# A hybrid decoder step on one core: a new opening, a second query tile in the residual loop, and a down projection that keeps the tokens stationary

## The chip, the cores and the metric

The kernel runs on one core of one Trainium2 chip (trn2). The metric is device time in microseconds; three runs of the kernel before gave 3130.1, 3130.15 and 3132.04 us, median 3130.15 us.

## What is computed

One layer of a decoder on 576 tokens: 512 prompt tokens and 64 sample tokens (8 sequences of 8). The width is 2048. Cut to what matters here:

```python
def decoder_layer(x, ...):
    h = rmsnorm(x, g_mix_pre)
    rq, rk, rv, rg, dq, dk, dv = mixer_projections(h, w_in, pos)   # 2048 -> 7168
    ...                                                            # retention and differential attention
    x = x + rmsnorm(mix @ w_out, g_mix_post)
    x = x + rmsnorm(cross_attn(rmsnorm(x, g_mem_pre), mem_k, mem_v, w_mem_q, w_mem_o), g_mem_post)
    x = x + rmsnorm(sq_relu_mlp(rmsnorm(x, g_mlp_pre), w_up, w_down), g_mlp_post)

def cross_attn(h, mk, mv, wq, wo):
    q = (h @ wq)                                                   # 2048 -> 4 heads of 128
    ...

def sq_relu_mlp(h, w_up, w_down):
    return jnp.square(jax.nn.relu(h @ w_up)) @ w_down              # 2048 -> 8192 -> 2048
```

All tensors are float32.

## The kernel before

The kernel is written engine by engine: one block each for SyncE (`sp`, weight loads and most stores), GpSimd (`pool`), ScalarE (`act`), VectorE (`dve`) and TensorE (`pe`). The order on each engine is the order of its text; semaphores with written-out counts tie them.

Products with weights are made from three float32r matmuls each: a float32 operand is split into a high part (a ScalarE copy into float32r) and a low part (a VectorE subtraction), and high times high, low times high and high times low are summed in PSUM (`parts`, L1846). Weights come in stripes of 128 x 2048 values (1 MB) through two buffers: SyncE loads `w_raw`, ScalarE writes `w_hi` (`hi`, L812; L1105 and L1118 in the MLP), VectorE writes `w_lo` (`lo`, L1165), and SyncE may load a buffer again when its `w_lo` is written. ScalarE may write `w_hi` of a buffer when TensorE has finished the tiles that read it.

Activations are kept transposed: features on partitions, the 576 tokens along the free axis. The weights are the stationary operand, the tokens the moving one, in two halves of 288 columns that go to two PSUM banks. An output tile is 128 features by 576 tokens. The PSUM banks are `G[0..3]` (gemm) and `A[0..3]` (aux).

The stages that the change touches:

- The opening. GpSimd loads the token tiles (`x_load`, L629) into two buffers `xin`, then four small lambda vectors and the page table; SyncE loads the constants and the first weight stripes at once; ScalarE's queue loads the gains. TensorE turns each token tile (`x_turn`, L1867), VectorE multiplies by the gain (L1189), ScalarE writes the high part (L832), VectorE the low part (L1196), in quarters of 512 columns. The gains themselves are turned once (L1888), after all small loads, the page table included. The first two input tiles are computed in halves (`half_tile`, L1875): half 0 of tile 0 after the third token tile, half 0 of tile 1, then five small matmuls that spread the norm factor, then both second halves.
- The residual after the mixer (`residual(0, ...)`, L1606 to L1615, with `first_tile` on TensorE). For each of 16 chunks VectorE makes the new x and its low part, ScalarE the high part and the square; TensorE sums the squares with two float32 matmuls (L2218, four instructions in the trace) and runs the six matmuls of the first query tile for that chunk. The other three query tiles follow, 96 matmuls each.
- The MLP, in 8 blocks of 1024 hidden features. `up` gives 8 tiles of hidden features: VectorE makes relu times the norm factor (L1755), ScalarE squares and writes `u_hi`, VectorE `u_lo` (L1760). `down` gives 16 tiles of output features of 8 chunks each, 8 stripes of 8 chunks x 256 columns; VectorE adds each tile to `yT` (L1777).
- The end. GpSimd loads the spilled x back over `act_hi` (L794) when the last up tile is done. In the last block squares of `yT` are summed over the tiles (L1143, L1592); then TensorE sums over partitions (L2208), ScalarE takes the root (L991), VectorE the reciprocal (L1596), VectorE and GpSimd scale `yT`, VectorE adds x (L1827), TensorE turns `yT` to tokens by features in 20 pieces (L1949), ScalarE and VectorE copy the pieces out of PSUM (L1150, L1817) and SyncE stores them (L614).

## Time and profile before

| | |
|---|---|
| median of 3 runs | 3130.15 us |
| profiled execution | 3132.76 us |
| its span, first to last instruction | 3131.1 us |
| TensorE (PE) busy | 3042.4 us (97%), 22485 matmuls |
| VectorE (DVE) busy | 1301.3 us (42%) |
| ScalarE (ACT) busy | 768.9 us (25%) |
| GpSimd (POOL) busy | 165.1 us (5%) |
| mean granted TensorE clock | 0.989 |
| DMA | 355.04 MB, mean 113 GB/s |

Times within the trace are microseconds from the span's start. PE's ends are modelled and successive matmuls overlap in the record, so the pace of a stream of matmuls is read from the distance of their starts, not from the length of one.

### The profile page before, as it was taken

To read this page: it belongs to the slowest core of one execution; us is meant where nothing else is said; L and a number is where in the kernel's file an instruction comes from. 1 tells how busy PE (TensorE), PEld (TensorE's weight loads), DVE (VectorE), ACT (ScalarE), POOL (GpSimd) and SP (SyncE) were. 2 spreads that over 40 slices of the span, in tenths; PEclk is the share of its full clock that TensorE was granted. 3 is DMA by queue.
4 is the path that set the end of the run, shared out by engine and by line. 5 is a ranking of instruction groups with operands and counts; after the bars stand their busy time and mean duration, and the time that the engine had idled before them with its cause. 6 is when DMAs were issued, how large, how long until landed. Compare 5 with 4: busy or idle time off the path is not lost.

```text
span 3131.1 us, 53528 instructions
## 1 busy us (share of the span) xinstructions
PE 3042.4 (97%) x22485; PEld 2931.0 (94%) x22485; DVE 1301.3 (42%) x1860; ACT 768.9 (25%) x836; POOL 165.1 (5%) x265
## 2 busy tenths in 40 slices
PE   7999999999999998998999999999999999999996
PEld 6899999989899997787999999999999999999995
DVE  6544245445554536467332322323323233232346
ACT  4311123223222233334212112122121121221221
POOL 0000012221211010000000000000000000000001
PEclk9999999999999999999999999999999999999997
DMA  5433535554656361513222223222222222222241
GB/s 181 156 103 107 151 117 162 167 168 149 218 162 222 134 211 54 148 55 115 81 80 81 91 73 89 82 80 80 80 80 86 77 87 86 80 80 80 80 141 61
DMA packets 398904, 355.04 MB, mean 113 GB/s; under 512 B 9554, under 2 KB 362052, under 8 KB 396772
## 3 DMA queue, kind: packets, MB, share of 16 engines
q1 hardware_dynamic: 377456, 269.18, 28.7%
q0 software_dynamic: 21136, 84.66, 7.9%
q8 instruction: 56, 0.92, 0.1%
q14 instruction: 28, 0.23, 0.0%
q10 hardware_dynamic: 228, 0.06, 0.0%
HBM read 305.62 MB, written 48.23 MB: 113 GB/s over the span
## 4 chain that ended last, share of the span: by engine, by line
PE 90%; issue 4%; DVE 3%; DMA 1%; POOL 1%; ACT 1%; DVEq 0%; POOLq 0%; ACTq 0%
PE gemm L1846 81%; PE aux L1949 2%; PE gemm L1926 1%; PE gemm L1875 1%; DVE yT L1606 1%; DVE yT L1827 1%; PE aux L1989 1%; PE aux L2005 1%; DMA d_vp<-in_cache_diff_v 0%; POOL d_kp L682 0%; POOL d_vp L682 0%; ACT w_hi L812 0%; DVE rstd_b L1596 0%; DMA pg<-in_page_table 0%; PE aux L2152 0%
## 5 line engine op out<-in xcount | busy, mean ns | idle before, releaser
L1846 PE MATMUL gemm<-act_hi,w_hi 128*128 128x288 f32 x4544 | 994.8, 300 | 7.8 <-DVE act_lo L1615 4.3
L1846 PE MATMUL gemm<-act_hi,w_lo 128*128 128x288 f32 x4544 | 973.4, 296 | 0.0
L1846 PE MATMUL gemm<-act_lo,w_hi 128*128 128x288 f32 x4544 | 972.7, 296 | 0.0
L1846 PEld LDWEIGHTS gemm<-act_hi,w_hi 128*128 128x128 f32 x4544 | 731.6, 189 | 41.2 <-issue 18.1
L1846 PEld LDWEIGHTS gemm<-act_lo,w_hi 128*128 128x128 f32 x4544 | 732.6, 189 | 0.0
L1846 PEld LDWEIGHTS gemm<-act_hi,w_lo 128*128 128x128 f32 x4544 | 732.6, 189 | 0.0
L1165 DVE TENSOR_TENSOR w_lo<-w_raw,w_hi 128x2048 fp32r<-128x2048 f32 x216 | 494.4, 2289 | 198.3 <-ACT w_hi L812 74.2
L1846 PE MATMUL gemm<-u_lo,w_hi 128*128 128x288 f32 x2048 | 438.6, 296 | 0.0
L1846 PE MATMUL gemm<-u_hi,w_hi 128*128 128x288 f32 x2048 | 438.5, 296 | 0.0
L1846 PE MATMUL gemm<-u_hi,w_lo 128*128 128x288 f32 x2048 | 438.4, 296 | 0.0
L1846 PEld LDWEIGHTS gemm<-u_hi,w_hi 128*128 128x128 f32 x2048 | 330.2, 189 | 0.0
L1846 PEld LDWEIGHTS gemm<-u_lo,w_hi 128*128 128x128 f32 x2048 | 330.2, 189 | 0.0
L1846 PEld LDWEIGHTS gemm<-u_hi,w_lo 128*128 128x128 f32 x2048 | 330.2, 189 | 0.0
L812 ACT ACTIVATE w_hi<-w_raw 128x2048 fp32r<-128x2048 f32 x90 | 172.1, 1912 | 335.8 <-PE gemm L1846 280.0
L1118 ACT ACTIVATE w_hi<-w_raw 128x2048 fp32r<-128x2048 f32 x63 | 120.8, 1918 | 516.6 <-PE gemm L1846 516.6
L1777 DVE TENSOR_TENSOR yT<-yT,gemm 128x288 f32 x192 | 78.5, 450 | 362.9 <-PE gemm L1846 362.9
L1755 DVE SCALAR_TENSOR_TENSOR z_out<-gemm,rstd_b 128x288 f32<-128x288 f32 x128 | 52.6, 452 | 405.1 <-PE gemm L1846 405.0
L1110 ACT ACTIVATE z_out<-z_out 128x576 f32<-128x576 f32 x64 | 43.9, 685 | 613.8 <-DVE z_out L1755 613.8
L1105 ACT ACTIVATE w_hi<-w_raw 128x2048 fp32r<-128x2048 f32 x63 | 120.1, 1906 | 77.4 <-PE gemm L1846 76.1
L794 POOL DMA_DIRECT2D act_hi<-x_scratch x1 | 0.6, 574 | 1818.6 <-PE gemm L1846 1818.6
L1760 DVE TENSOR_TENSOR u_lo<-z_out,u_hi 128x576 f32 (+1 forms) x64 | 48.5, 758 | 112.4 <-ACT u_hi L1112 112.4
L1235 DVE TENSOR_TENSOR z_out<-gemm,rstd_b 128x288 f32<-128x288 f32 x48 | 19.7, 451 | 99.1 <-PE gemm L1846 99.1
(309 smaller groups left out, 1922.9 us busy)
## 6 DMA issues: line engine op xcount, KB each, us to landing
w_raw<-in_w_mlp_up SPq DMA_DIRECT2D x64, 1024.0 KB, 6.4
w_raw<-in_w_mlp_down SPq DMA_DIRECT2D x64, 1024.0 KB, 5.3
w_raw<-in_w_in SPq DMA_DIRECT2D x56, 1024.0 KB, 5.7
w_raw<-in_w_out SPq DMA_DIRECT2D x16, 1024.0 KB, 6.0
z_scratch<-z_out SPq DMA_DIRECT2D x56, 288.0 KB, 2.1
r_zin<-z_scratch POOLq DMA_DIRECT2D x8, 1152.0 KB, 6.3
xin<-in_x_prompt POOLq DMA_DIRECT2D x8, 1024.0 KB, 6.8
d_z<-z_scratch POOLq DMA_DIRECT2D x12, 576.0 KB, 7.1
```

The costliest lines, as they stand in the source:

```text
L812: nc.scalar.activation(w_hi[b][:], w_raw[b][:], ACT.Copy).then_inc(s_whi, 1)
L1105: nc.scalar.activation(w_hi[(b + 1) % 2][:], w_raw[(b + 1) % 2][:], ACT.Copy).then_inc(s_whi, 1)
L1110: nc.scalar.activation(u_s[:], u_t[:], ACT.Square).then_inc(u_sq, 1)
L1118: nc.scalar.activation(w_hi[(b + 1) % 2][:], w_raw[(b + 1) % 2][:], ACT.Copy).then_inc(s_whi, 1)
L1165: V.tensor_tensor(w_lo[b][:], w_raw[b][:], w_hi[b][:].bitcast(F32), ALU.subtract).then_inc(s_wlo, 1)
L1606: V.tensor_tensor(y, y, n_rt[:], ALU.mult).then_inc(n_t, 1)
L1755: ins = V.scalar_tensor_tensor(out=u_t[:, cols], in0=G[2 * b + half][:, 0:TH], scalar=0.0, in1=rstd_b[:, cols], op0=ALU.max, op1=ALU.mult)
L1760: V.tensor_tensor(u_lo[:, k, :].rearrange("p a t -> p (a t)"), u_s[:], u_hi[:, k, :].rearrange("p a t -> p (a t)").bitcast(F32), ALU.subtr ...
L1777: ins = V.tensor_tensor(y, y, G[2 * m + half][:, 0:TH], ALU.add)
L1827: V.scalar_tensor_tensor(out=yT[:, c, :], in0=yT[:, c, :], scalar=gT[:, G_MLP_POST + c:G_MLP_POST + c + 1], in1=x_back[:, c, :], op0=ALU.m ...
L1846: ins = M(out[half][:, 0:TH], w[b][:, cols], x[:, k, half * TH:(half + 1) * TH], start=first and n == 0, stop=last and n == 2)
L1949: return nc.tensor.transpose(out, in_, ident[0:rows, 0:rows])
```

## The change

Four parts, in one kernel:

- Opening: five token buffers in place of two, so that the five token tiles are issued at once; the lambda vectors go to SyncE's queue and the page table gets its own semaphore; SyncE starts the weight stripes after the first token tile has landed; the gain of the first norm is loaded first and turned alone; ScalarE's squares come later than its high parts; half 1 of tile 0 goes ahead of the five small matmuls.
- Residual: the second query tile runs in the loop, four chunks behind the first (`first_tiles`); tiles 2 and 3 use other banks (`q_bank`).
- Down projection: 128 tokens of `u_hi` or `u_lo` are the stationary operand and 512 columns of weights the moving one. Each block has 4 column blocks of 512 and each of these 5 units, 128 prompt tokens each and, third in order, the 64 sample tokens, whose high and low part stand side by side as one stationary operand. A column block needs two stripes of 4 chunks x 512 columns; the units' five banks stay open over both.
- End: `y_tok` holds tokens by features, so the norm is a sum along the row. The gain is a row (`g_row`) that GpSimd loads after x, over `act_lo`. VectorE waits for it before the last block's down projection. TensorE turns x in place of y, three of the 20 pieces ahead of the last column block.

```diff
@@ sync
             sp.dma_start(cst[:], cst_d).then_inc(s_cst, 16)
+            for k, v in enumerate((lq1, lk1, lq2, lk2)):
+                sp.dma_start(g_rows[G_LAM + k:G_LAM + k + 1, :], v).then_inc(s_lam, 16)
+            sp.wait_ge(s_xin[0], 16)
             for n in range(EARLY):
...
-                        w_load(sp, None, b, down_v[bass.ds(f, 1), :, :, bass.ds(i * (4 * P) + b * (2 * P), 2 * P)]
-                               .rearrange("a p k n -> p (a k) n"), FC)
+                        w_load(sp, None, b, down_v[bass.ds(f, 1), :, 4 * b:4 * b + 4, bass.ds(i * 512, 512)]
+                               .rearrange("a p k n -> p (a k) n"), 4)
@@ gpsimd
-            x_load(0)
-            x_load(1)
-            for k, v in enumerate((lq1, lk1, lq2, lk2)):
-                pool.dma_start(g_rows[G_LAM + k:G_LAM + k + 1, :], v).then_inc(s_lam, 16)
-            pool.dma_start(pg[:], pages.rearrange("(a b) n -> a (b n)", a=1)).then_inc(s_lam, 16)
+            for p in range(NT):
+                x_load(p)
+            pool.dma_start(pg[:], pages.rearrange("(a b) n -> a (b n)", a=1)).then_inc(s_pg, 16)
...
             pool.dma_start(x_back, x_d).then_inc(s_back, 16)
-
-            pool.wait_ge(n_rcp, 5)
-            with pool.Fori(0, KC // 2) as i:
-                scale(2, 2 * i + 1)
+            pool.dma_start(g_row[:], g_mlp_post.to_broadcast([P, D])).then_inc(s_grow, 16)
@@ scalar, residual(k, ...)
+                if k == 0:
+                    hi(stripe + 2, 0, stripe % 2, tile + EXTRA + 1)
                 for half in range(2):
                     act.wait_ge(n_used, (k + 1) * KC + 2)
@@ scalar, last block
+                for q, t in enumerate(d_units):
                     rows = tok(t)[1]
-                    n = NT * q + t
-                    act.wait_ge(s_yt, n + 1)
-                    nc.scalar.activation(y_tok[t][0:rows, q * 512:(q + 1) * 512], A[n % 4][0:rows, :], ACT.Copy).then_inc(s_ytc[0], 1)
+                    act.wait_ge(f_sum, NT * j + q + 1)
+                    nc.scalar.activation(z_out[0][0:rows, 0:512], y_tok[t][0:rows, j * 512:(j + 1) * 512], ACT.Square,
+                                         accum_out=y_ssq[0:rows, t, j:j + 1]).then_inc(f_ssq, 1)
+                    if j == DJ - 1 and q:
+                        row_root(d_units[q - 1], q - 1)
@@ vector, down
             def down(f):
-                with dve.Fori(0, FC // 2) as i:
+                with dve.Fori(0, DJ) as j:
                     for b in range(2):
-                        lo(S_MLP + FC + 1 + b, (b + 1) % 2, f * MLP_STRIPES + 2 * i)
-                        for m in range(2):
-                            down_tile(f, i, b, m)
+                        lo(S_MLP + FC + 1 + b, (b + 1) % 2, f * MLP_STRIPES + 2 * j)
+                    for q in range(NT):
+                        down_unit(f, j, q)
@@ vector, last block and end
+            dve.wait_ge(s_grow, 16)
+            for j in range(DJ):
+                for b in range(2):
+                    if 2 * j + b < FC - 1:
+                        lo(S_MLP + (FB - 1) * MLP_STRIPES + FC + 1 + 2 * j + b, (b + 1) % 2)
+                for q in range(NT):
+                    last_unit(j, q)
+                    if j == DJ - 1:
+                        row_sum(q)
+                    gain(j, q)
+                    if j == DJ - 1 and q:
+                        row_factor(q - 1)
+            row_factor(NT - 1)
+            for q in range(NT):
+                result(q)
@@ tensor, residual
+                for c in range(KC):
+                    pe.wait_ge(n_xsq, c + 1)
+                    for half in range(2):
+                        ins = M(A[2 + half][:, 0:TH], ones[:], n_sq[c % 2][:, half * TH:(half + 1) * TH], start=c == 0, stop=c == KC - 1)
+                    ins.then_inc(n_used, 1)
+                    if c >= behind:
+                        chunk(1, c - behind)
+                    pe.wait_ge(n_lo, c + 1)
+                    ins = chunk(0, c)
+                ins.then_inc(s_tile, 1)
+                for c in range(KC - behind, KC):
+                    ins = chunk(1, c)
@@ tensor, down
+            def down_stripe(f, j, b, last=False):
+                pe.wait_ge(s_wlo, f * MLP_STRIPES + 2 * j + (S_MLP + FC + b + 1))
+                pe.wait_ge(u_l, f * FC + (4 * b + 5))
+                for q, t in enumerate(d_units):
+                    before = q - NT + 1 if t < PC else 0
+                    if b == 0 and last and j:
+                        pe.wait_ge(f_sum, NT * j + before)
+                    elif b == 0:
+                        pe.wait_ge(s_evac, f * MLP_TILES + NT * j + (G_MLP + FC + before))
+                    for k in range(4):
+                        c, cols = 4 * b + k, slice(k * 512, (k + 1) * 512)
+                        if t < PC:
+                            hi, lo = u_hi[:, c, t * P:(t + 1) * P], u_lo[:, c, t * P:(t + 1) * P]
+                            M(A[t][:], hi, w_hi[b][:, cols], start=c == 0, stop=False)
+                            M(A[t][:], lo, w_hi[b][:, cols], start=False, stop=False)
+                            ins = M(A[t][:], hi, w_lo[b][:, cols], start=False, stop=c == FC - 1)
+                        else:
+                            M(G[2][:], u_hi[:, c, TP:T + TS], w_hi[b][:, cols], start=c == 0, stop=False, skip_group_check=True)
+                            ins = M(G[2][0:TS, :], u_hi[:, c, TP:T], w_lo[b][:, cols], start=False, stop=c == FC - 1,
+                                    skip_group_check=True)
+                    if b:
+                        ins.then_inc(s_tile, 1)
+                    elif q == NT - 1:
+                        ins.then_inc(s_down, 1)
```

In `result` VectorE makes, for each of the 20 pieces of 512 columns, one scalar_tensor_tensor: the row times its factor plus the turned x from PSUM.

## Rows read from the trace of the kernel before

**Rows 1.** The page: the chain that ended last, by engine.

```profile
PE 90%; issue 4%; DVE 3%; DMA 1%; POOL 1%; ACT 1%; DVEq 0%; POOLq 0%; ACTq 0%
```

**Rows 2.** Busy time by stretch: length, PE, PEld, DVE, ACT, POOL, PEclk, DMA share, GB/s.

```profile
1458.00:3084.00 1626.00, 1626.00 (x12196) 1625.93 (x12195) 509.02 (x589) 333.27 (x271) 0.57 (x1) 1.00 0.29 85
3084.00:3131.00 47.00, 17.75 (x91) 15.08 (x89) 36.99 (x36) 8.82 (x15) 14.46 (x8) 0.65 0.29 101
```

**Rows 3.** The chain that ended last, pieces in order: start, length, what.

```profile
4.68 10.02 DMA pg<-in_page_table
...
36.84 7.96 PE gemm L1875 x48
...
45.94 6.52 PE gemm L1875 x48
...
67.32 1.75 PE aux L1867 x16
...
1458.42 1626.39 PE gemm L1846 x12198
```

**Rows 4.** Timeline of PE, 512-column matmuls of the memory keys; 160 left out.

```profile
104.59 0.39 PE L1926 MATMUL gemm<-w_hi,mem_hi 128*128 128x512 f32 x1
...
141.08 0.39 PE L1926 MATMUL gemm<-w_lo,mem_hi 128*128 128x512 f32 x1
```

**Rows 5.** Landing times: first token tile; the one issued at 23.33; first weight stripe.

```profile
DMA to landing us min/median/max: 8.5/8.5/8.5
...
DMA to landing us min/median/max: 5.1/5.1/5.1
...
DMA to landing us min/median/max: 13.3/13.3/13.3
```

**Rows 6.** Timeline of the opening: start, length, engine, line, operation.

```profile
15.83 1.41 DVE L1189 TENSOR_TENSOR gx<-aux,gT 128x512 f32<-128x512 f32 x2
...
21.89 1.42 DVE L1189 TENSOR_TENSOR gx<-aux,gT 128x512 f32<-128x512 f32 x2
...
26.29 1.43 DVE L1196 TENSOR_TENSOR act_lo<-gx,act_hi 128x512 fp32r<-128x512 f32 x2
...
26.82 1.89 ACT L812 ACTIVATE w_hi<-w_raw 128x2048 fp32r<-128x2048 f32 x1
...
28.75 2.29 DVE L1165 TENSOR_TENSOR w_lo<-w_raw,w_hi 128x2048 fp32r<-128x2048 f32 x1 [1.04 <-ACT w_hi L812]
```

**Rows 7.** Timeline of PE in the residual loop after the mixer.

```profile
1233.79 1.13 PE L2218 MATMUL aux<-z_out,ones 128*128 128x288 f32 x4
...
1235.56 1.13 PE L2218 MATMUL aux<-z_out,ones 128*128 128x288 f32 x4
...
1240.71 0.53 PE L1846 MATMUL gemm<-act_hi,w_hi 128*128 128x288 f32 x2 [0.22 <-DVE act_lo L1615]
...
1261.47 0.64 PE L1846 MATMUL gemm<-act_hi,w_hi 128*128 128x288 f32 x2
```

**Rows 8.** The load of x in the last block: its issue, its time to landing.

```profile
2983.00 0.57 POOL L794 DMA_DIRECT2D act_hi<-x_scratch  x1 [1818.64 <-PE gemm L1846]
...
DMA to landing us min/median/max: 14.4/14.4/14.4
```

**Rows 9.** The end (timeline), the stores (DMA issues), a 512-column operation on PSUM (line).

```profile
3084.84 0.82 DVE L1807 TENSOR_TENSOR yT<-yT,gemm 128x288 f32<-128x288 f32 x2 [4.07 <-PE gemm L1846]
3085.70 0.68 ACT L1143 ACTIVATE z_out<-yT 128x576 f32<-128x576 f32 x1 [5.71 <-DVE yT L1807]
...
out<-xT SPq DMA_DIRECT2D x16, 256.0 KB, 2.6
...
L1189 DVE TENSOR_TENSOR gx<-aux,gT x28: 424/691/693, 15.8 to 91.9; 128x512 f32<-128x512 f32 x24, 128x256 f32<-128x256 f32 x4
```

**Rows 10.** Waits of 1290 to 1420 (total, times, longest); loads of down stripes (us to landing).

```profile
PE gemm L1846 <- DVE yT L1585: 3.5, 4, 2.2
...
w_raw<-in_w_mlp_down SPq DMA_DIRECT2D x64, 1024.0 KB, 5.3
```

More of the change, by code:

```diff
@@ L818, in _, with x_square @@
             act.dma_start(g_rows[G_SUB:G_SUB + 2, :], subln.rearrange("a (c p) -> (a c) p", p=P)).then_inc(s_gain, 16)
+            def x_square(p):
+                t = order[p]
+                rows = x_tiles[t][1]
+                act.wait_ge(s_xin[p % NT], 16 * (p // NT + 1))
+                act.wait_ge(e_act.sem, e_act.before("sq", p))
+                e_act.did(nc.scalar.activation(sq_junk[0:rows, :], xin[p % NT][0:rows, :], ACT.Square,
+                                               accum_out=ssq[0:rows, t:t + 1]), "sq")
             def x_norm(p):
@@ L1626, in residual @@
                 low(k, KC - 1, g_pre)
+                if k == 0:
+                    lo(stripe + 2, stripe % 2)
                 dve.wait_ge(n_rts, 4 * k + 4)
@@ new lines, in gain, with row_sum @@
+            def gain(j, q):
+                t = d_units[q]
+                cols = slice(j * 512, (j + 1) * 512)
+                rows = tok(t)[1]
+                y = y_tok[t][0:rows, cols]
+                dve.wait_ge(f_ssq, NT * j + q + 1)
+                step(V.tensor_tensor(y, y, g_row[0:rows, cols], ALU.mult))
+            def row_sum(q):
+                t = d_units[q]
+                rows = tok(t)[1]
+                dve.wait_ge(f_ssq, NT * (DJ - 1) + q + 1)
+                V.tensor_reduce(y_rms[0:rows, t:t + 1], y_ssq[0:rows, t, :], AX.X, ALU.add).then_inc(f_add, 1)
@@ new lines, in row_factor, with result @@
+            def row_factor(q):
+                t = d_units[q]
+                rows = tok(t)[1]
+                dve.wait_ge(f_rms, q + 1)
+                step(V.reciprocal(y_rms[0:rows, t:t + 1], y_rms[0:rows, t:t + 1]))
+            def result(q):
+                t = d_units[q]
+                rows = tok(t)[1]
+                settled()
+                for j in range(DJ):
+                    n = DJ * q + j
+                    y = y_tok[t][0:rows, j * 512:(j + 1) * 512]
+                    dve.wait_ge(s_xtok, n + 1)
+                    V.scalar_tensor_tensor(out=y, in0=y, scalar=y_rms[0:rows, t:t + 1], in1=x_bank[n % 8][0:rows, :],
+                                           op0=ALU.mult, op1=ALU.add).then_inc(f_out, 1)
@@ L2222, in first_tile, with first_tiles, chunk @@
                 ins.then_inc(s_tile, 1)
+            def first_tiles(stripe, tile, behind):
+                pe.wait_ge(s_wlo, stripe + 2)
+                pe.wait_ge(s_evac, tile)
+                def chunk(m, c):
+                    return parts((stripe + m) % 2, c, slice(c * P, (c + 1) * P), act_hi, act_lo, G[2 * m:2 * m + 2], c == 0, c == KC - 1)
+                for c in range(KC):
[11 more added lines that the diff above has]
+                ins.then_inc(s_tile, 1)
             def out_tile(n):
@@ L2398, in down @@
             def down(f):
[L2399 removed]
+                with pe.Fori(0, DJ) as j:
                     for b in range(2):
[L2401 to L2406 removed]
+                        down_stripe(f, j, b)
@@ L2408, in _, with x_piece @@
+            def x_piece(n):
+                q, j = n // DJ, n % DJ
+                c0, rows = tok(d_units[q])
+                if n >= 8:
+                    pe.wait_ge(f_out, n - 7)
+                for jj in range(4):
+                    ins = turn(x_bank[n % 8][0:rows, jj * P:(jj + 1) * P], x_back[:, 4 * j + jj, c0:c0 + rows])
+                ins.then_inc(s_xtok, 1)
             first_tile(1, S_MLP, G_MLP)
@@ L2413, in _ @@
             down(0)
-            with pe.Fori(1, FB) as f:
+            with pe.Fori(1, FB - 1) as f:
                 with pe.Fori(0, FC // 2) as i:
```

313 lines of the change are left out of this document (166 added, 147 removed).

## Prediction, made before the changed kernel ran

> **What bounds the kernel now.** First the page: TensorE carries 90% of the chain that ended last [rows 1]. Then the busy time by stretch: from 1458 to 3084, the MLP, TensorE has no idle time at all at the full clock, with VectorE busy for 509 of 1626 us; in the last 47 us it is busy for 17.75 and its granted clock is 0.65 [rows 2]. So the MLP can only be shortened by giving TensorE less time's worth of matmuls, and the end, the opening and the residual loops by shortening chains of other engines. Third, the pieces of the chain: the MLP is one piece of 12198 matmuls in 1626.39 us, so a matmul of 288 columns starts every 0.1333 us [rows 3]. That is 320 cycles of 2.4 GHz for 288 columns. The 512-column matmuls of the memory keys start every 36.49/161 = 0.2266 us [rows 4], which is 544 cycles. Both pay 32 cycles beyond their columns, and both load a new stationary operand each time. This is the price list for the down projection.
>
> **Down projection, TensorE.** Before, a block has 16 tiles x 8 chunks x 6 = 768 matmuls: 768 x 0.1333 = 102.4 us. After, a block has 4 column blocks x 8 chunks x (4 units x 3 + 2) = 448 matmuls of 512 columns: 448 x 0.2266 = 101.5 us. Eight blocks: -6.9 us. The streamed columns rise (221184 to 229376 per block); the 32 cycles that 320 instructions no longer pay win it back. One in seven of the new matmuls (64 of 448) has either both halves of the sample tokens or 64 of them stationary; no row shows that form with float32r, and I take the same pace, as its columns are the same. Bounds: +27.3 us for the eight blocks if only columns counted (8192 more per block at 2.4 GHz), and -6.9, as no row shows a 512-column matmul at less than 0.2266.
>
> What feeds it is covered. A stripe lasts 56 x 0.2266 = 12.7 us (12.8 before). ScalarE's part is 1.9 us and VectorE's 2.3 us [rows 6] after the buffer is free, a stripe lands in 5.3 us [rows 10]. VectorE is queued in the order: split of the next stripe, which waits for ScalarE, which waits for the first stripe's end; then five additions of 0.7 us [rows 9]. The split is done 4.3 us into the second stripe, the first unit is finished at 2.7 and is needed again at 12.7. The wait of the third unit for all additions of the column block before falls 5.4 us after the last unit ended, against 0.8 us for its addition. I cost these at nothing.
>
> A sentence from the Trainium skill (TensorE: Matmul & The Clock Gate, Back-to-back issue gap) speaks against this part: a warm matmul is said to cost its columns at 2.4 GHz plus 2.5 ns. By that figure a block would go from 768 x 122.5 = 94.1 us to 448 x 215.8 = 96.7 us, 2.6 us longer, and eight blocks would lose 21 us. The trace has 133.3 ns and 226.6 ns, so I go by the trace.
>
> **Opening.** In the chain the page table's load, last in GpSimd's queue behind two token tiles, takes 10.02 us, and the norm begins at 15.83 after it [rows 3, 6]. After the change it begins when the first token tile is there. That load took 8.5 us beside weights and a second tile, and a tile issued alone 5.1 us [rows 5]; nothing but constants and small rows now run beside it, so I take 5.3: issue 1.5, landing 6.8, one quarter turned in 0.9, norm from 7.8. A tile's norm takes VectorE 27.7 - 21.9 = 5.8 us [rows 6]. Three tiles, 0.9 us for the lambdas (at most the 1.1 us between the page table's landing and 15.83) and 0.8 us where ScalarE's split of a stripe delays its high parts: 26.9. One split of 2.3 us follows, and half 0 of tile 0 can start at 29.8 with the semaphores, in place of 36.84. All that follows to 67.32 keeps its length (7.96 + 6.52 for the half tiles, and so on), as VectorE's fourth tile (31.9 + 5.8 = 37.7) is ready when the first half tile ends. So -7.0 us. The new risk is DMA: five tiles (4.5 MB) stand in GpSimd's queue beside two stripes. The first stripe took 13.3 us beside two tiles [rows 5]; issued at 6.9 it lands at 20.2, just when ScalarE gets to it (20.1). If it gets less of the engines beside four tiles, every microsecond is lost in the start. Bounds: -3 to -9. Moved past others: SyncE issues four lambda rows and waits before its stripes; GpSimd's later work is due much later.
>
> The Trainium skill (DMA: Bandwidth & Descriptors, Arbitration) says that a DMA engine takes turns between queues by packets; the token rows are the bigger packets, so by it the stripes get the smaller share. It would move the sum towards the -3.
>
> **Residual.** In the loop TensorE is the slower side for the first chunks: sums and six matmuls take 1235.56 - 1233.79 = 1.77 us; later it waits 0.22 us for VectorE's low part in each chunk [rows 7]. Six more matmuls cost 0.80, so a chunk takes 2.57 us from the fifth on. The loop's first tile ends at 1261.47 + 0.80 = 1262.3 before, and at 1235.56 + 12 x 2.57 = 1266.4 after: +4.1. Then four chunks of the second tile, +3.2. The third tile's stripe can be split only when the first tile is done: 1.9 + 2.3 + 0.1 = 4.3 us, of which 3.2 are covered: +1.1. The second tile alone, 96 x 0.1333 = 12.8 us, is gone. Together -4.4 us (bounds -6, if the loop keeps VectorE's pace, and -3).
>
> **Last block.** A new wait: VectorE waits for the gain row before the first split of the last down projection. GpSimd issues it behind x, after the last up tile; x took 14.4 us from 2983.0, with one stripe of 1 MB beside it [rows 8]. The gain row is another 1 MB, and the stripe's next load is behind the waiting split, so x and gain land together at about 2998 to 2999. Queued behind the wait is the split of the second stripe; TensorE gets to it 12.7 us after the up tiles, at 2995.3, and it is ready at 2998.5 + 2.3 = 3000.8. That is +5.5 us (bounds 2 and 9). The clock then is low for a while: the first half tile in the opening took 7.96 us against 6.52 for the second [rows 3], so +1.6. Twelve transposes for three pieces of x lie on TensorE's path: 12 x 0.11 [rows 3] = +1.3.
>
> **End.** Before: from the last matmul's addition at 3084.84 to 3131.1, 46.3 us [rows 9]. After, in the last column block, a prompt unit costs VectorE 0.7 (addition) + 0.8 (ScalarE's square and row sum of 512 columns; 0.68 for 576 without the sum [rows 9]) + 0.7 (gain) + 0.3 (row sum and factor) = 2.5 us, the sample unit with two more additions 4.0 us. It gets units at 2.7, 5.4, 7.3, 10.0 and 12.7 and is done with them at 17.1, 4.4 us after TensorE. Then 20 pieces of x plus scaled y at 0.72 each [rows 9], 14.4 us, as TensorE can turn pieces eight ahead; then the last store, 2.6 us [rows 9]. 21.5 us, with the semaphores, in place of 46.3: -24.8. The stores run at 256 KB per 0.72 us behind it; if they are slower, the end grows by up to 5 us. Gone are the reciprocal over 576 columns, the scaling in two engines and the alternating copies.
>
> **Sum.** -7.0 - 4.4 - 6.9 + 5.5 + 1.6 + 1.3 - 24.8 = -34.7 us. Against the profiled execution's own 3132.76 us that is 3098.1; that execution is 2.6 us above the median of the three runs, so the forecast for the median is 3095.5.
>
> **The rivals.**
> Weights late in the opening: the first stripe waits for the token tiles; the opening gives 3, and the time is 3099.5. For it: the 13.3 us of the first stripe; against: it came to ScalarE early enough by my estimate.
> A worse last block: gain row at 3003 or stores below VectorE's pace, +8 us: 3103.5.
> A better one: gain row at 2995, loop at VectorE's pace, token tile at 6.6: 3089.
> The down projection does not save what it should, since the 32 cycles belong to the columns or to the loads rather than to the instruction: then 8192 more columns cost 3.41 us a block, 34.2 us against my sum in all, and the time is 3129.7. Against it: both widths show 32 cycles.
> Slower than before: eviction behind the split. The third unit of each column block waits for additions that VectorE makes after a split. In the cross-attention's output the same order made TensorE wait for VectorE's evictions four times, up to 2.2 us [rows 10]. Were it 2.2 us in each of 32 column blocks, 70.4 us would come back: 3165.9. It decides from 1.08 us per column block. Against it: 5.4 - 0.8 = 4.6 us of slack by the times above.
>
> **How the numbers follow.** Forecast 0.55; late weights 0.15; worse last block 0.12; better 0.10; columns only 0.03; evictions 0.05. The first four lie from 3085 to 3109, with the bounds of the opening, the stall and the end; the rest is left out. A measurement of this kernel tells 0.2%, some 6 us, from no change: faster 0.91 (3123.9 or less), same 0.04, slower 0.05.
>
> **What would show it.** In the down stretch matmul starts 0.227 us apart without idle time; the first half tile near 30; chunks of 2.57 us in the residual loop; one idle time of TensorE near 5.5 us in the last block whose releaser is a VectorE split, with VectorE idle before it until the gain row's load; about 21 us from the last matmul to the end. I am wrong if 64-row units run at another pace, if TensorE shows idle time at each column block, or if the end is paced by the stores.

## The result, and the profile of the changed kernel

| | before | after |
|---|---|---|
| median of the runs | 3130.17 us | 3105.14 us (3102.87 to 3106.08) |
| ratio, with its 95% interval | 1 | 0.9917 (0.9905 to 0.9929) |
| profiled execution | 3132.76 us, span 3131.1 | 3104.61 us, span 3102.9 |
| mean granted TensorE clock | 0.989 | 0.989 |

The kernel is 25.0 us faster. 34.7 were forecast, so the time lies inside the range of 3085 to 3109 but 9.6 us above the forecast of 3095.5. To see which term missed, I cut both spans at the same five points of the program and compared the lengths. The two spans differ by 28.1 us; the other 3.1 us of the way to the medians are no part of the change, as the profiled execution of before was 2.6 us above its median and that of after 0.5 us below its own.

| stretch, and the starts that bound it | before | after | difference | forecast |
|---|---|---|---|---|
| opening, to the last matmul of the memory keys (141.08 and 139.74) | 141.1 | 139.7 | -1.3 | -7.0 |
| mixer, to the row sums after it (1215.03 and 1212.73) | 1074.0 | 1073.0 | -1.0 | 0 |
| residual and cross-attention, to the first low part of the MLP's products (1465.47 and 1457.08) | 250.4 | 244.4 | -6.1 | -4.4 |
| MLP, to the last up tile's second VectorE operation (2982.91 and 2970.85) | 1517.4 | 1513.8 | -3.7 | -6.0 |
| the last block's down projection, to its last matmul (3084.51 and 3082.06) | 101.6 | 111.2 | +9.6 | +7.5 |
| end (3131.06 and 3102.93) | 46.6 | 20.9 | -25.7 | -24.8 |

The forecast's -6.9 for the pace stands here as 7/8 in the MLP and 1/8 in the last block. The largest miss by far is the opening.

**The opening.** These are pieces of the chain that ended last, of the kernel after (start, length, what), then one row of its timeline; [rows 3, 6] are their counterparts.

```profile
1.48 6.57 DMA xin<-in_x_prompt
...
8.06 18.37 DMA w_raw<-in_w_in
...
26.46 1.91 ACT w_hi L824
28.37 0.53 ACT act_hi L850
...
33.32 2.21 DVE w_lo L1202
...
35.57 7.86 PE gemm L1951 x48
```

```profile
28.99 0.69 DVE L1228 TENSOR_TENSOR act_lo<-gx,act_hi 128x512 fp32r<-128x512 f32 x1 [6.12 <-ACT act_hi L850]
```

The page table is gone from the chain, as forecast. The first token tile took 6.57 us to land, where 5.3 were forecast. In the page table's place stands a transfer of 18.4 us: the first weight stripe lands at 26.4, not at 20.2. ScalarE waits for it with the third tile's high parts (`act_hi`) queued behind, VectorE stands idle for 6.12 us until the first of these is made, and the first half tile starts at 35.57 (36.84 before, 29.8 forecast). Where the stripe's bytes were is in the DMA queues' rows (packets, MB, share of 16 engines), here from 8.0 to 13.2 us, while the second and third token tile land; q0 carries GpSimd's transfers, q1 SyncE's:

```profile
q0 software_dynamic: 289, 2.11, 97.5%
q1 hardware_dynamic: 62, 0.03, 2.0%
```

For five microseconds after its issue the stripe got 0.03 MB of the 2.16 MB that were moved, and none of its packets moved before 11.5 us. After that the queues took turns, one packet for one: the first rows below are those of the kernel after from 12 to 16 us, the second those of the kernel before from 7 to 11.

```profile
q0 software_dynamic: 176, 1.29, 98.2%
q1 hardware_dynamic: 165, 0.08, 8.8%
```

```profile
q0 software_dynamic: 213, 1.42, 89.0%
q1 hardware_dynamic: 211, 0.11, 9.3%
```

A token tile's packet has 7.3 KB here (1.29 MB in 176), a stripe's 0.5. So beside tiles a stripe hardly moves, and most of it moves when they are through: from 20 to 22 us SyncE's queue, nearly alone, moved 1143 packets, 0.58 MB. Then the first memory tile, issued at 16.90, set it back once more (94 packets to 109 from 23 to 25 us, 0.77 MB to 0.06), ahead of the landing at 26.4. In the kernel before it had such a stretch at the start. The tiles, issued at 1.50, had their first bytes just before 5 us, and from 2 to 5 us SyncE's queue moved 1414 packets, 0.84 MB, against 2 of GpSimd's. That is what stands behind the even shares of the kernel before from 1.8 to 10 us:

```profile
q0 software_dynamic: 219, 1.66, 52.2%
q1 hardware_dynamic: 1892, 1.09, 50.0%
```

**The residual loop.** Timeline of TensorE; the counterpart is [rows 7].

```profile
1234.56 1.13 PE L2315 MATMUL aux<-z_out,ones 128*128 128x288 f32 x4
...
1237.12 1.13 PE L2315 MATMUL aux<-z_out,ones 128*128 128x288 f32 x4
...
1267.15 0.53 PE L1922 MATMUL aux<-act_hi,w_hi 128*128 128x288 f32 x2 [1.20 <-DVE w_lo L1202]
```

A chunk takes 2.56 us (2.57 forecast), VectorE's low part is no longer waited for in the loop, and behind it the third tile waits 1.20 us for its stripe's split (1.1 forecast).

**The pace, the stall and the end.** Busy time by stretch (columns as in [rows 2]): the whole MLP to the last matmul, and the end.

```profile
1450.04:3082.30 1632.26, 1626.09 (x9652) 1468.97 (x9651) 522.19 (x573) 336.84 (x296) 1.12 (x2) 1.00 0.28 85
3082.30:3102.93 20.63, 10.21 (x69) 6.88 (x67) 15.54 (x28) 1.69 (x7) 0.00 (x0) 0.85 0.64 230
```

TensorE is idle for 6.17 us of the 1632, and all of it is one gap. Timeline of PE, one sample unit between the units around it, in a block before the last:

```profile
1750.01 0.39 PE L2521 MATMUL gemm<-w_hi,u_hi 128*128 128x512 f32 x1
1750.24 0.40 PE L2522 MATMUL gemm<-w_lo,u_hi 128*64 128x512 f32 x1
...
1751.63 0.40 PE L2522 MATMUL gemm<-w_lo,u_hi 128*64 128x512 f32 x1
1751.86 0.39 PE L2517 MATMUL aux<-w_hi,u_hi 128*128 128x512 f32 x1
```

The prompt units run at 0.2266 us per matmul (1746.16 to 1749.79 is 16 of them), the price taken in the forecast. In the sample unit every second matmul has only the 64 sample tokens stationary (`128*64` in the row: 64 rows of the result instead of 128). Its eight matmuls take 1.85 us, 0.2313 each on average. A block's down part takes 101.89 us where 101.5 were forecast.

The gap, in the chain, in VectorE's timeline and in TensorE's:

```profile
2971.51 15.39 DMA g_row<-in_norm_mlp_post
```

```profile
2986.93 4.49 DVE L1202 TENSOR_TENSOR w_lo<-w_raw,w_hi 128x2048 fp32r<-128x2048 f32 x2 [13.02 <-DMA g_row<-in_norm_mlp_post]
...
2989.28 0.80 PE L2517 MATMUL aux<-w_hi,u_hi 128*128 128x512 f32 x1 [6.17 <-DVE w_lo L1202]
```

The gain row lands with x 15.4 us after its issue. Two splits follow back to back, and with the first of them TensorE can go on, after 6.17 us of standing (5.5 forecast). Then its clock is low; busy time by stretch of the gap and of what follows:

```profile
2983.10:2989.30 6.20, 0.03 (x2) 0.03 (x1) 2.37 (x2) 1.91 (x1) 0.00 (x0) 0.86 0.40 169
2989.30:2995.00 5.70, 5.70 (x15) 4.55 (x16) 2.45 (x2) 0.00 (x0) 0.00 (x0) 0.56 0.78 263
```

The granted clock is 0.56 there, most of it at the lower of the two levels, 1.2 GHz. From the starts below the matmuls run at full pace again, the first in this kernel, the second in the half tile of the kernel before, from which the forecast took its price:

```profile
2994.48 0.39 PE L2517 MATMUL aux<-w_hi,u_hi 128*128 128x512 f32 x1
```

```profile
40.03 0.30 PE L1875 MATMUL gemm<-act_lo,w_hi 128*128 128x288 f32 x1
```

From the first start behind the gap, at 2989.28, to 2994.48 twelve matmuls take 5.20 us, where 12 x 0.2266 = 2.7 is the full pace: 2.5 us lost, where 1.6 were forecast. In the half tile thirteen matmuls took from 36.84 to 40.03, 3.2 us, where 13 x 0.1333 = 1.7 is the full pace. The end, from VectorE's last addition on (counterpart [rows 9]):

```profile
3083.38 0.66 DVE L1848 TENSOR_TENSOR y_tok<-y_tok,aux 128x512 f32<-128x512 f32 x1
...
3085.76 2.06 DVE L1883 SCALAR_TENSOR_TENSOR y_tok<-y_tok,y_rms,gemm 128x512 f32<-128x512 f32 x3
...
3098.27 0.73 DVE L1883 SCALAR_TENSOR_TENSOR y_tok<-y_tok,y_rms,aux 128x512 f32<-128x512 f32 x1
```

TensorE begins its last turns at 3082.30 and VectorE the results 3.5 us later (4.4 forecast); 20 results take 13.2 us, 0.66 each (0.72 forecast); from the last one's end at 3099.0 it is 3.9 us to the end of the span (2.6 forecast).

### The profile page after: what moved, and what is told of

It is laid out like the page before. It is cut to its first block, busy times and chain, and to the rows that moved or that the text cites. A ratio compares the mean times of both kernels' runs of the same rounds, so it can differ in the third digit from the quotient of the medians.

```text
span 3102.9 us, 48144 instructions
## 1 busy us (share of the span) xinstructions
PE 3028.3 (98%) x19922; PEld 2763.9 (89%) x19922; DVE 1293.1 (42%) x1837; ACT 765.7 (25%) x853; POOL 149.5 (5%) x254
## 4 chain that ended last, share of the span: by engine, by line
PE 93%; DVE 2%; issue 2%; DMA 2%; ACT 1%; POOL 0%; DVEq 0%; ACTq 0%; POOLq 0%
PE gemm L1922 57%; PE aux L2517 7%; PE aux L2518 7%; PE aux L2519 7%; PE gemm L2522 2%; PE gemm L2521 2%; PE aux L2028 2%; PE gemm L2005 1%; PE gemm L1951 1%; DMA w_raw<-in_w_in 1%; PE aux L2068 1%; PE aux L2084 1%; PE aux L2315 1%; DMA g_row<-in_norm_mlp_post 0%; DVE w_lo L1202 0%
## 5 line engine op out<-in xcount | busy, mean ns | idle before, releaser
L2517 PE MATMUL aux<-w_hi,u_hi 128*128 128x512 f32 x1024 | 400.0, 391 | 6.2 <-DVE w_lo L1202 6.2
L2518 PE MATMUL aux<-w_hi,u_lo 128*128 128x512 f32 x1024 | 399.4, 390 | 0.0
L2519 PE MATMUL aux<-w_lo,u_hi 128*128 128x512 f32 x1024 | 399.3, 390 | 0.0
L2517 PEld LDWEIGHTS aux<-w_hi,u_hi 128*128 128x128 f32 x1024 | 192.9, 188 | 49.9 <-DVE w_lo L1202 6.6
L2519 PEld LDWEIGHTS aux<-w_lo,u_hi 128*128 128x128 f32 x1024 | 192.8, 188 | 40.6
L2518 PEld LDWEIGHTS aux<-w_hi,u_lo 128*128 128x128 f32 x1024 | 192.8, 188 | 40.1
L1821 DVE TENSOR_TENSOR y_tok<-y_tok,aux 128x512 f32 x96 | 65.9, 686 | 114.3 <-PE aux L2519 114.3
L2522 PE MATMUL gemm<-w_lo,u_hi 128*64 128x512 f32 x256 | 101.4, 396 | 0.0
L2521 PE MATMUL gemm<-w_hi,u_hi 128*128 128x512 f32 x256 | 99.7, 390 | 0.0
L1804 DVE TENSOR_TENSOR u_lo<-z_out,u_hi 128x512 f32 (+1 forms) x64 | 44.3, 692 | 115.2 <-ACT u_hi L1140 115.2
```

Source lines behind the costliest of these rows:

```text
L1821: ins = V.tensor_tensor(y, y, y_bank[t][:], ALU.add)
L2517: M(A[t][:], hi, w_hi[b][:, cols], start=c == 0, stop=False)
L2518: M(A[t][:], lo, w_hi[b][:, cols], start=False, stop=False)
L2519: ins = M(A[t][:], hi, w_lo[b][:, cols], start=False, stop=c == FC - 1)
L2521: M(G[2][:], u_hi[:, c, TP:T + TS], w_hi[b][:, cols], start=c == 0, stop=False, skip_group_check=True)
L2522: ins = M(G[2][0:TS, :], u_hi[:, c, TP:T], w_lo[b][:, cols], start=False, stop=c == FC - 1, skip_group_check=True)
```

## The experiments

Medians of kernels that ran in different series can be compared to about 1.5 us, as the medians of the kernel before in the four series, 3130.5 to 3131.7, and the runs of one kernel, often 3 us apart, show. Where a stretch can be read from the traces, I go by that.

### One part at a time

The kernel before with one part of the change each: its opening, its residual loop, its down projection with the end.

> The kernel before with the new opening alone. Theory (the two weight stripes, the five token tiles and the first memory tile share a DMA that is full from 8 to 26.5 us, so the opening gives back most of its gain): first half tile near 35.6 us, 1.4 us gained up to the mixer, 3127.8 to 3128.8. Rival (the opening is worth the forecast 7 us and another part of the change takes it back): first half tile near 30, 3123.2.

> The kernel before with the second query tile in the residual loop alone. Theory (the trace after, 5.7 us between the row sums and the MLP): 3124.5. The forecast's own term: 4.4 us, 3125.8. Rival (the loop's gain depends on the other parts, for instance on where VectorE stands): within 1 us of 3130.2.

> The kernel before with the token-stationary down projection and its new end alone. Theory (the trace after: 4.2 us from the matmul's pace, 19.8 us with the end and the stall for the gain row): 3110.4 to 3112.3, with the same stall of 6.2 us in the last block. The forecast's own terms: 23.3 us, 3106.9. Rival (the stall comes from the state the new opening or the residual leave): no stall, near 3103.

| | median (range), runs | ratio, 95% interval | against 3130.62 |
|---|---|---|---|
| opening | 3129.17 (3124.48 to 3132.19), 10 | 0.9993 (0.9983 to 1.0003) | -1.4 |
| residual | 3125.75 (3124.82 to 3126.83), 10 | 0.9985 (0.9976 to 0.9995) | -4.9 |
| down and end | 3111.69 (3110.29 to 3114.53), 4 | 0.9941 (0.9924 to 0.9958) | -18.9 |

Together 25.2 us, and the change with all three gave 25.0: to the 1.5 us above, the parts add, and none takes back what another gives. The stall is there with the down projection alone (6.44 us). The residual loop came where the forecast's own term put it (3125.8), not at the 3124.5 of my theory. The opening can't be told from no change, and its runs spread over 7.7 us. The profiled one (3125.96) is one of the short ones: its first stripe landed at 22.8, 15.5 us after its issue, and the first half tile started at 31.95, neither the 35.6 of the theory nor the 30 of the rival. That the landing differs so from run to run would explain the spread; one profiled run of each can't show it. In the residual stretch these traces also correct my reading of before: the three kernels of this section and a later one that have the old or new loop give

| loop | length of the stretch, us |
|---|---|
| old: before; down_only; open_only; open_held | 250.4; 248.3; 247.6; 247.5 |
| new: after; resid_only | 244.4; 244.7 |

and 2 to 3 us of the 6.1 above belong to the one execution of before that was profiled. The eight other kernels below with the new loop give 242.9 to 244.6. The mean of the ten with the new loop is 243.9, that of the three old ones without before 247.8: by the traces the loop is worth 3.9 us.

### The opening: what the stripe waits for

First, the tiles that are not needed yet step back, in GpSimd's program:

```
             for p in range(NT):
+                if p == 3:
+                    pool.wait_ge(s_wfull[0], 16)
                 x_load(p)
```

> The changed kernel with GpSimd waiting, behind the third token tile, until the first weight stripe has landed; the fourth and fifth tile, the page table, a constant and the first memory tile come behind it. Theory (the stripe is late because the tiles share a full DMA with it; bytes: 2.3 to 3.3 MB at 379 GB/s from 8.06): the first stripe lands at 14 to 17 us instead of 26.4, the first half tile starts at 30.5 instead of 35.6, VectorE's norm being what it waits for, 3100. Rival (its rows of 512 bytes take 13.3 us whatever is beside them, as in the kernel before): it lands at 21.4, the first half tile still at 30.5. Rival (the opening is bound by something else): 35.6 and 3105.

3101.85 us (3097.32 to 3102.34), ratio 0.9902 (0.9886 to 0.9919). Pieces of its chain, and its queues from 13.3 to 20.3 us:

```profile
1.48 5.92 DMA xin<-in_x_prompt
...
20.04 1.80 ACT w_hi L826
...
29.04 7.98 PE gemm L1953 x48
```

```profile
q1 hardware_dynamic: 3132, 1.59, 90.2%
q0 software_dynamic: 72, 0.59, 24.4%
```

The stripe landed at 16.65, 9.2 us after its issue instead of 18.4, and the first half tile started at 29.04, 0.8 us before the forecast of the prediction. That is the theory, and against "its rows of 512 bytes take 13.3 us whatever is beside them". SyncE's queue moved nothing from 7.9 to 11 us, as in the kernel after, but then the three tiles were through: from 12 to 16.6 us it moved 2672 packets, 1.36 MB, against 6 of GpSimd's. The keys' last matmul came 6.4 us earlier than in the kernel after, but the median fell by only 3.3 us: in this trace 3.6 us are lost again between 490 and 700 us, at three of the attention's page loads. Two kernels below with the same opening lost 0.3 and 1.4 us from the keys to the row sums, and the next one, whose transfers are those of the kernel after, lost 1.5. So the loss is not shown to be the edit's; what sets the landing of those loads was not tried and stays open.

Second, the order alone, with every transfer as it was:

```
+            x_norm(2)
             hi(0, 0, 0, None)
-            x_norm(2)
             hi(1, 0, 1, None)
```

> The changed kernel with ScalarE splitting the two stripes behind the third tile's high parts instead of ahead of them; no transfer is changed. Theory (part of the loss is order: ScalarE waits for the stripe with the third tile's high parts queued behind it, and VectorE waits for those): the stripe lands at 26.4 as before, VectorE's norm of three tiles ends near 27.2, the low part of the stripe is made from 28.4 to 30.6, the first half tile starts at 30.7, 3100.2. Rival (the landing alone counts): 35.6, 3105.

3100.95 us (3099.37 to 3103.07), ratio 0.9905 (0.9888 to 0.9921). Pieces of its chain:

```profile
26.36 1.81 ACT w_hi L824
28.19 2.30 DVE w_lo L1202
30.54 7.88 PE gemm L1951 x48
```

The stripe still landed at 25.96, but the third tile's norm was done by then. So the late landing costs 6.5 us only because ScalarE's program waits for it in front of work that VectorE needs; behind that work, the same landing costs 1.5 us.

Third, the stripes issued at once, with SyncE's `sp.wait_ge(s_xin[0], 16)` left out:

> The changed kernel without SyncE's wait for the first token tile, so that the stripes are issued at 2 us. Theory: the first stripe lands at 13 to 16, the first token tile at 10.0 as before the change instead of 8.05, the norm starts at 11.3, the first half tile at 32.3, 3101.8. Rival (six megabytes in front of the third tile make that tile late): third tile behind 20 us, first half tile at 35 or later, 3105 or more.

3105.51 us (3104.7 to 3107.0), ratio 0.9919 (0.9903 to 0.9936): no gain, and my expectation was wrong in its main number. Issued at 2.56 instead of 8.06, the stripe landed at 26.33 instead of 26.44. The first token tile was not delayed either (7.66). From 2.6 to 8.0 us the queues were

```profile
q0 software_dynamic: 215, 1.63, 80.9%
q1 hardware_dynamic: 123, 0.10, 5.5%
```

so the stripe's issue 5.5 us earlier bought it 0.1 MB at most. Its queue's packets came behind 6.6 us, and from 7 to 16 us the queues moved 442 packets (3.23 MB) and 439 (0.22 MB), one for one again. Fourth, the stripes ahead of everything on SyncE, as before the change:

```
+            for n in range(2):
+                w_load(sp, n, ...)
             for k, v in enumerate((lq1, lk1, lq2, lk2)):
                 sp.dma_start(g_rows[G_LAM + k:G_LAM + k + 1, :], v)...
-            sp.wait_ge(s_xin[0], 16)
```

> The changed kernel with the first two weight stripes issued by SyncE ahead of the four lambda rows and without the wait for the first token tile, so ahead of the token tiles as in the kernel before. Theory A (what is issued first keeps its share: before, the stripes' queue had 50% and the tiles' 52% until 10 us): the first stripe lands at 14 to 16, the first token tile at 10, the first half tile starts at 31 to 32, 3101.5. Theory B (the number of tiles that stand in the other queue decides: five after, two before): the stripes' queue gets under 10% until 13 us, the stripe lands at 26, the first half tile starts at 35.5, 3105.

3115.24 us (3114.56 to 3116.29), ratio 0.995 (0.9933 to 0.9966): 10 us slower than the kernel after, which neither theory gave. The queues answered the question all the same, from 1.3 to 10 us and from 7 to 17 us:

```profile
q0 software_dynamic: 245, 1.88, 54.0%
q1 hardware_dynamic: 1615, 0.95, 39.4%
...
q0 software_dynamic: 500, 3.60, 95.1%
q1 hardware_dynamic: 497, 0.25, 9.2%
```

Neither theory says what happens. Issued ahead of the tiles, SyncE's queue has the engines nearly alone until the tiles' first bytes come (1276 packets to 13 from 2 to 5 us), and its 39.4% is mostly that head start. From then on the queues go packet for packet, as with two tiles in the kernel before and as with the tiles issued first in the kernel after. The first stripe landed at 21.91. What made the kernel slower is a piece of its chain:

```profile
14.10 13.98 issue
28.08 0.43 PE gemm L1967
```

TensorE stands for 14 us in front of the transpose of the gains and lambdas. The profile names no releaser. By the program it waits for the gains, in ScalarE's queue, which moved nothing more after 14 us, and for the four lambda rows of half a KB each, which now stand behind 2 MB of stripes. SyncE's issue of the first of them, at 3.64, took 17.4 us, and the other three were issued from 21.09 to 21.66:

```profile
L507 SPq DMA_DIRECT2D g_rows<-in_diff_lambda_q x2: 253/8828/17404, 3.6 to 21.4; - x2
```

So it is the lambda rows that are late. The prediction had noted that SyncE issues them ahead of its stripes, and had not said what that is worth: it is worth 8 us of the first half tile (35.57 against 43.64).

Last, the new opening alone again, now with the tiles held:

> The kernel before with the new opening alone, and in it the fourth token tile and all behind it held until the first weight stripe has landed. Theory (the share of the DMA is the one thing that the opening's term missed, and it also makes the runs of the opening alone spread over 8 us): first stripe landed by 17, first half tile at 29 to 30, 3122.8 to 3124.5, all runs within 3 us. Rival (what the opening gains is lost at the page loads of the attention, which come at their own time): first half tile at 29 to 30, but 3127 or more. Rival (the spread has another cause): runs spread over 6 us or more again.

3121.98 us (3120.9 to 3124.98), 6 runs, ratio 0.9969 (0.9956 to 0.9981) against 3131.66 us in its series: 9.7 us, by the interval 6 to 14. The stripe landed at 16.53, the first half tile started at 28.95, 7.9 us before that of the kernel before. By the traces 6.5 us are gained up to the last matmul of the keys (134.62 against 141.08). So the opening is worth what was forecast once the stripe has its share, and the rival that the page loads take the gain back (3127 or more) is out. The runs spread over 4.1 us instead of 7.7. That is more than the 3 us I expected, but no more than the kernel before spreads by itself (4.2 us in 19 runs, 4.6 in 9).

### The last block: the wait for the gain row

The first edit issues the gain row ahead of x on GpSimd, the second leaves the transfers and moves VectorE's wait behind its first two splits:

```
+            pool.dma_start(g_row[:], ...).then_inc(s_grow, 16)
             pool.dma_start(x_back, x_d).then_inc(s_back, 16)
-            pool.dma_start(g_row[:], ...).then_inc(s_grow, 16)
```

> The changed kernel with the gain row's transfer issued ahead of x instead of behind it. Theory (VectorE waits for the gain row, which lands with the 4.6 MB of x, and the second stripe's split is queued behind that wait): the gain row lands within 8 us, TensorE has no idle time in the last block and no low clock after it, 3096.2 to 3098. Rival (the split is late because the second stripe's own transfer or ScalarE is late beside x): idle time stays, 3105.

```
-            dve.wait_ge(s_grow, 16)
             for j in range(DJ):
                 for b in range(2): ... lo(...)
+                if j == 0:
+                    dve.wait_ge(s_grow, 16)
```

> The changed kernel with VectorE's wait for the gain row moved behind the splits of the first two stripes; the transfers stay in their order. Theory (the stall is the split queued behind the wait; the gain row itself is not needed until the first unit's product): the gain row still lands near 2987, but the splits start at 2975 and 2985, TensorE has no idle time, 8.8 us less than the changed kernel in the stretch, 3096.3 to 3098.4. Rival (the row is late for the first product too, and the additions behind it hold TensorE): 1 to 4 us of idle time remain, 3100 to 3102.

| | median (range) | ratio, 95% interval |
|---|---|---|
| gain row first | 3098.38 (3096.59 to 3099.63) | 0.9897 (0.9881 to 0.9914) |
| wait later | 3097.35 (3095.02 to 3100.91) | 0.9893 (0.9876 to 0.9909) |

VectorE's timeline, of the one and of the other:

```profile
2977.04 2.29 DVE L1202 TENSOR_TENSOR w_lo<-w_raw,w_hi 128x2048 fp32r<-128x2048 f32 x1 [1.95 <-DMA g_row<-in_norm_mlp_post]
2986.33 2.29 DVE L1202 TENSOR_TENSOR w_lo<-w_raw,w_hi 128x2048 fp32r<-128x2048 f32 x1 [6.99 <-ACT w_hi L1149]
```

```profile
2976.63 2.29 DVE L1202 TENSOR_TENSOR w_lo<-w_raw,w_hi 128x2048 fp32r<-128x2048 f32 x1 [0.86 <-ACT w_hi L1149]
2987.01 2.29 DVE L1202 TENSOR_TENSOR w_lo<-w_raw,w_hi 128x2048 fp32r<-128x2048 f32 x1 [8.09 <-ACT w_hi L1149]
2990.06 0.69 DVE L1848 TENSOR_TENSOR y_tok<-y_tok,aux 128x512 f32<-128x512 f32 x1 [0.76 <-DMA g_row<-in_norm_mlp_post]
```

In both, TensorE has no wait in the last block, and from its first down matmul to its last it takes 103.0 us instead of 111.9 (gain row first: 2971.36 to 3074.39). The 8.8 us are the gap of 6.17 and 2.7 of low clock, by difference; 2.5 of these are in the rows above. With the wait moved, the gain row is late by 0.76 us only, and nothing that TensorE needs waits for that addition. So the mechanism is the one of the prediction, a split queued behind a wait that it doesn't need, and either edit cures it.

### The pace of the sample unit

The sample unit's second matmul of each chunk takes the high and low halves as stationary operand, 128 rows of the result, instead of the 64 high ones; the product low by low comes on top.

```
-  ins = M(G[2][0:TS, :], u_hi[:, c, TP:T], w_lo[b][:, cols], ...)
+  ins = M(G[2][:], u_hi[:, c, TP:T + TS], w_lo[b][:, cols], ...)
```

> The changed kernel with the sample unit's second matmul taking all 128 rows of the stationary operand (high and low halves) instead of 64, which adds the low by low product. Theory (the 64-row form costs 0.231 us per pair instead of 0.2266): a sample unit's eight matmuls take 1.813 us instead of 1.85, the down part of a block 101.5 us instead of 101.9, 3.1 us in all, 3102.0. Rival (the extra belongs to the change of the PSUM bank or of the moving operand): no change, 3105.

3103.05 us (3101.9 to 3103.53), ratio 0.9909 (0.9893 to 0.9926). Timeline of PE, the start of a sample unit and the matmul behind its end:

```profile
1751.36 0.39 PE L2521 MATMUL gemm<-w_hi,u_hi 128*128 128x512 f32 x1
...
1753.18 0.39 PE L2517 MATMUL aux<-w_hi,u_hi 128*128 128x512 f32 x1
```

Eight matmuls take 1.82 us instead of 1.85, and a block's down part 101.57 instead of 101.89. With 32 such matmuls in a block, one with 64 rows costs 0.010 us more than one with 128, though it does less: 2.6 us over the eight blocks, almost all of the 2.8 that the pace lacked. The bank and the moving operand are as before, so the rival is out. (The 0.231 us of the expectation is for one matmul, not for a pair.) Here narrow and wide ones always alternate; whether the price is of the width or of the change between widths was not tried.

### The three edits together

Tiles held, gain row first, sample unit at full width.

> The changed kernel with three edits of the earlier runs together: the fourth token tile and all behind it held until the first stripe has landed, the gain row issued ahead of x, and the sample unit's second matmul over all 128 rows. Theory (they touch different stretches and add): 3105.1 - 3.3 - 6.8 - 2.1 = 3092.9, first half tile at 29, no idle time of TensorE in the last block. Rival (x, now last, becomes late for the turns in front of the last column block, or the opening's gain is lost at the page loads): 3096 or more.

3087.56 us (3086.3 to 3090.26), ratio 0.9862 (0.9846 to 0.9879), 17.6 us below the kernel after and 42.9 below that of before. By the traces the edits are worth 6.3 us (first half tile at 29.27 instead of 35.57), 8.8 and 2.6, which is 17.7: they add. I had expected 5 us less since I had taken the opening at the 3.3 us of its own median. Busy time by stretch, the MLP to the last matmul, in which TensorE now has no idle time:

```profile
1451.00:3064.90 1613.90, 1613.90 (x9599) 1473.96 (x9598) 517.51 (x570) 334.60 (x293) 1.12 (x2) 1.00 0.28 85
```

## Why the prediction was right, and where it was not

The parts, their places and their directions were those of the forecast, but the time is nearer to two of the rivals (late weights at 3099.5, a worse last block at 3103.5) than to 3095.5. What missed most is the opening: its forecast of -7.0 failed as late weights, which had a chance of 0.15.

- **Opening: -7.0 forecast, -1.3 came.** The steps on VectorE were right in sum: with the stripe in time the first half tile starts at 29.0 (29.8 forecast), though the first token tile lands at 7.4 there and not at 6.8. The step that failed is "issued at 6.9 it lands at 20.2". I had taken 13.3 us from the kernel before, where the stripe went out ahead of two tiles, and used it for a stripe behind four. There its queue had three microseconds nearly to itself before the tiles' first bytes came, and here the tiles came first. It measured 18.4. The risk was named ("if it gets less of the engines beside four tiles, every microsecond is lost in the start"), and so was the order on ScalarE (0.8 us for its split), but I gave the rival 0.15 and bounded it at -3. It ended past that bound. The total of the bytes could have told it: 4.5 MB of tiles, 2 MB of stripes and 1 MB of memory at the 343 GB/s that the kernel before moved from 1.8 to 10 us take 22 us (an estimate), so what gets the smaller share lands past 20. The row that I held against this rival rested on the landing that was in question.
- The Trainium skill (DMA: Bandwidth & Descriptors, Arbitration) says that an engine takes turns between queues by packets. The trace agrees, wherever both queues have packets to move: 176 to 165 in the kernel after, 213 to 211 in the kernel before, 442 to 439 and 500 to 497 in two of the experiments. With 7.3 KB in GpSimd's packets and 0.5 KB in SyncE's, the stripes got a sixteenth of the bytes, 0.02 MB a microsecond in the kernel after, and moved 0.29 alone. The 52% and 50% of the kernel before are no exception, but the mean of a stretch alone and of turns behind it. I let the sentence move the sum "towards the -3" and no chance with it, and it is what happened.
- **Residual: -4.4 forecast, -4.9 (-1.6 to -7.5) measured alone, -3.9 by the traces.** The chunk of 2.57 us came as 2.56, the wait of 1.1 as 1.20.
- **Pace: -6.9 forecast, -4.1 came** (0.51 us x 8). The mechanism is right: each matmul of 512 columns costs 0.2266 us, so the columns are not all that counts (rival at 3129.7 out), and the 21 us that the eight blocks would have lost by the quoted formula did not come. The 64-row form was named as one that no row shows and priced like its neighbour; it costs 0.010 us more. That is one of the prediction's own signs of being wrong ("if 64-row units run at another pace"); it came true, and is worth 2.6 us.
- **Last block: +8.4 forecast for stall, clock and turns, +10.2 came** (8.8, and 1.4 for the turns, 103.03 less the 101.66 from the first to the last matmul of a block without them). Mechanism and place were right to the row; the gap was 6.17 instead of 5.5. The clock cost 2.7 instead of 1.6, since it held for 5.2 us of matmuls and not for the 3.2 of the half tile from which I took it. (The 1.6 is 7.96 less 48 x 0.1333; less the 6.52 that the prediction names it is 1.4.)
- **End: -24.8 forecast, -25.7 came.** The results came at 0.66 us instead of 0.72 (1.2 us in 20), the handover 0.9 us sooner, and 1.3 us were lost behind the last result. The prediction's sign "if the end is paced by the stores" is not excluded for these: 256 KB per 0.66 us are 397 GB/s, and the DMA engines moved about 380 while they were busy with the stores. Nothing was tried on it.
- **Evictions behind the split** (3165.9) is out: TensorE has one idle time in the MLP, and none at a column block.
- **The median.** I carried the gain of one execution over to the median. That execution was 2.6 us above the median, and the traces of three other kernels show 2 to 3 us too much in its residual stretch. This was no term of mine, and it flatters the first table's stretches by as much. Of the 9.6 us between forecast and measured median 6.6 are in the spans (34.7 against 28.1), and the rest is that the profiled executions differ by 3.1 us more than the medians.

## What to carry to other kernels

When a change makes more transfers start together, add up the bytes that must land before the first use and divide by what the full DMA moves. Then compare the packets: beside packets of 7.3 KB those of 0.5 KB went one for one and got a sixteenth of the bytes. Such a transfer lands last, whatever it took in other company, and issuing it some microseconds sooner may buy nothing. Holding back what is not needed yet does. And on each in-order engine, put no wait in front of work that another engine needs first: the same late landing cost 6.5 us in front of such work and 1.5 us behind it, and the wait for the gain row 8.8 us or nothing.

## What the runs showed of the hardware that I had not expected

- A matmul of 512 columns with 64 rows of result costs 0.010 us more than one with 128, in a row where the two alternate (a block's down part, with 32 of them, took 101.89 us, and 101.57 us without).
- Where two DMA queues both had packets to move, they went packet for packet: 213 to 211 (kernel before, 7 to 11 us), 176 to 165 (after, 12 to 16 us), 442 to 439 (stripes at once), 500 to 497 (stripes first). Rows of 0.5 KB beside rows of up to 8 KB moved 0.02 to 0.03 MB a microsecond, and 0.29 nearly alone (after, 20 to 22 us). Neither the order of issue nor the number of tiles in the other queue changed this.
- From a stripe's issue beside token tiles to the first packets of its queue 3.4 us passed (8.06 to 11.5) and 4.0 (2.56 to 6.6, stripes at once).
- Four rows of 0.5 KB behind 2 MB of the same queue held TensorE for 14 us; SyncE's issue of the first of them alone took 17.4 us.
